# Projections for the gated recurrence taken inside it, in units of 128 columns, one head ahead

## What is computed

```python
    q_l, k_l, v_l, r_f, r_b, z_gla = ...            # 4 heads, dk 128, dv 256; z_gla 1024 wide
    la = log_sigmoid(r @ w_decay + b_decay) / 16    # per direction
def step(s, inp):                                    # _gla_scan, chunked
    bcum = jnp.cumsum(ac, axis=2)
    o_inter = jnp.einsum('bhtd,bhde->bhte', qc * jnp.exp(bcum), s)
    att = jnp.einsum('bhtd,bhsd,bhtsd->bhts', qc, kc, decay)
    o_intra = jnp.einsum('bhts,bhse->bhte', att, vc)
    s_new = jnp.exp(b_last[:, :, 0, :])[..., None] * s + jnp.einsum('bhsd,bhse->bhde', kc * jnp.exp(b_last - bcum), vc)
    br_c = (_rmsnorm(gla_o, gla_g_l).reshape(b_, t_, GLA_DV) * jax.nn.silu(z_gla)) @ w_br_gla_l
```

## Time and profile before

| | us |
|---|---|
| runs, median of 3 (range) | 2614.88 (2614.45 to 2615.42) |
| the profiled execution, device time | 2613.92 |
| its span, first to last instruction | 2612.1 |
| PE busy in the span | 2375.4 (91%) |
| DVE, ACT busy | 1527.6, 960.3 |

### The profile page before, as it was taken

How to read it: one execution, slowest core, us unless ns; L and a number is a source line. 1 busy time by engine, 2 the same in 40 slices (tenths; PEclk the granted TensorE clock), 3 DMA queues, 4 the chain that set the end, 5 groups by cost and what they waited for, 6 DMA issues and landing times.

```text
span 2612.1 us, 33657 instructions
## 1 busy us (share of the span) xinstructions
PE 2375.4 (91%) x13234; PEld 2070.6 (79%) x13234; DVE 1527.6 (58%) x2790; ACT 960.3 (37%) x1493; POOL 30.6 (1%) x37
## 2 busy tenths in 40 slices
PE   8899999999999777699988999998997669979997
PEld 6789988789888677688866888887786659949996
DVE  7879967789964355542344434454443455455665
ACT  5654535655442233222223321222333324334342
POOL 0000000000000000000000000000000100000000
PEclk9899989999989777799978999999998679989998
DMA  5258746178743100023210333332231005405552
GB/s 191 81 175 267 255 129 195 51 232 262 231 162 90 47 1 1 2 81 97 81 33 2 98 96 96 99 97 95 65 111 44 1 1 158 133 0 154 174 181 89
DMA packets 154709, 284.60 MB, mean 109 GB/s; under 512 B 9460, under 2 KB 34164, under 8 KB 154296
## 3 DMA queue, kind: packets, MB, share of 16 engines
q1 hardware_dynamic: 152448, 276.60, 34.0%
q10 hardware_dynamic: 2104, 5.85, 0.6%
HBM read 281.37 MB, written 1.05 MB: 108 GB/s over the span
## 4 chain that ended last, share of the span: by engine, by line
PE 75%; DVE 14%; DVEq 4%; ACT 4%; issue 2%; DMA 1%; ACTq 0%; SPq 0%
PE bank L1713 19%; PE bank L1714 19%; PE bank L1715 19%; DVE WLO L845 3%; PE bank L2065 2%; PE bank L2064 2%; PE bank L2117 1%; PE bank L1918 1%; PE bank L2134 1%; PE bank L2226 1%; PE bank L2246 1%; PE bank L2143 1%; DVEq L1261 1%; DVE ARENA L1258 1%; DMA RAW<-in_e_w_in 1%
## 5 line engine op out<-in xcount | busy, mean ns | idle before, releaser
L845 DVE TENSOR_TENSOR WLO<-RAW,WHI 128x1024 fp32r<-128x1024 f32 (+2 forms) x500 | 583.3, 1172 | 614.0 <-ACT WHI L453 601.9
L453 ACT ACTIVATE WHI<-RAW 128x1024 fp32r<-128x1024 f32 (+2 forms) x500 | 508.0, 1017 | 1092.9 <-PE bank L1715 1063.7
L1713 PE MATMUL bank<-ATH,WHI 128*128 128x256 f32 (+1 forms) x2032 | 655.3, 322 | 7.2 <-DVE ARENA L1400 2.6
L1714 PE MATMUL bank<-ATL,WHI 128*128 128x256 f32 (+1 forms) x2032 | 652.6, 321 | 0.0
L1715 PE MATMUL bank<-ATH,WLO 128*128 128x256 f32 (+1 forms) x2032 | 652.4, 321 | 0.0
L1713 PEld LDWEIGHTS bank<-ATH,WHI 128*128 128x128 f32 x2032 | 388.0, 191 | 40.0 <-DVE h L900 2.2
L1714 PEld LDWEIGHTS bank<-ATL,WHI 128*128 128x128 f32 x2032 | 387.9, 191 | 28.4
L1715 PEld LDWEIGHTS bank<-ATH,WLO 128*128 128x128 f32 x2032 | 387.8, 191 | 28.1
L1713 PE MATMUL bank<-WHI,ATH 128*128 128x512 f32 (+2 forms) x772 | 297.0, 385 | 12.3 <-DVE WLO L845 5.1
L1714 PE MATMUL bank<-WLO,ATH 128*128 128x512 f32 (+2 forms) x772 | 293.8, 381 | 0.0
L1715 PE MATMUL bank<-WHI,ATL 128*128 128x512 f32 (+2 forms) x772 | 293.2, 380 | 0.0
(11 more groups left out here) (277 smaller groups left out, 2820.8 us busy)
## 6 DMA issues: line engine op xcount, KB each, us to landing
RAW<-in_w_in SPq DMA_DIRECT2D x192, 512.0 KB, 3.6
RAW<-in_w_ff SPq DMA_DIRECT2D x128, 512.0 KB, 4.8
ARENA<-in_w_ada SPq DMA_DIRECT2D x64, 384.0 KB, 5.0
RAW<-in_o_w_in SPq DMA_DIRECT2D x24, 512.0 KB, 3.8
RAW<-in_e_w_in SPq DMA_DIRECT2D x16, 512.0 KB, 4.8
RAW<-in_w_ple_gate SPq DMA_DIRECT2D x16, 512.0 KB, 3.9
RAW<-in_w_br_gla SPq DMA_DIRECT2D x16, 512.0 KB, 3.5
RAW<-in_w_br_attn SPq DMA_DIRECT2D x16, 512.0 KB, 3.5
```

What stands on the lines that cost most here:

```text
L453: nc.scalar.activation(WHI[:, slot, 0:n], RAW[:, slot, 0:n], ACT.Copy).then_inc(hi_split, 1)
L845: V.tensor_tensor(WLO[:, slot, 0:n], RAW[:, slot, 0:n], WHI[:, slot, 0:n], ALU.subtract).then_inc(lo_split, 1)
L1713: mm(o, ah, bh, start=start, stop=False, skip_group_check=free)
L1714: mm(o, ah, bl, start=False, stop=False, skip_group_check=free)
```

## The change

It replaces the segments gq, gv and zg by a segment gh of five quads. Quads 0 to 3 belong to one head each: slot 0 holds 128 columns of q weights over all 1024 rows, slots 1 and 2 the head's 256 columns of v weights (512 rows each), slot 3 128 columns of z weights. Quad 4 holds the other four units of z. PE computes a unit of columns in two halves of 12 matmuls (`columns`) and values in four tiles of 24 (`value_tile`) in banks 2 and 3, placed by hand between the steps of the head before. ACT copies each piece out of PSUM (`taken`, semaphore piece_out), where DVE did so. z goes to ZRAW unactivated, its sigmoids are taken in a row behind the recurrence, and DVE forms silu, the products and the splits (`gate_z`) beside the first two quads of mgc. The GLA now has banks 0 and 1 for tiles and levels (4 to 7 for scores, states and outputs), turns rows into banks 6 and 7, and runs a head's turn and levels 0 to 2 before the head before it has ended; a level's scores run up to two levels behind its sums.

```diff
+    def tall(w, c0):
+        return (w, (lambda i: 0), (lambda i: c0), KC, P)
+
+    def head(w, i):
+        values = [(w, (lambda _, r=r: r * D // 2), (lambda _: C_GV + i * GDV), KC // 2, GDV) for r in range(2)]
+        return [tall(w, C_GQ + i * GDK)] + values + [tall(w, C_ZG + i * P)]
...
-            (f"gk{n}", 1, [std(w, C_GK)]), (f"gq{n}", 1, [std(w, C_GQ)]), (f"gr{n}", 1, [std(w, C_R, width=P)]),
-            (f"gv{n}", 2, [std(w, C_GV, BLK)]), (f"zg{n}", 2, [std(w, C_ZG, BLK)]),
+            (f"gk{n}", 1, [std(w, C_GK)]), (f"gr{n}", 1, [std(w, C_R, width=P)]),
+            (f"gh{n}", 1, [head(w, i) for i in range(GH)] + [[tall(w, C_ZG + (GH + u) * P) for u in range(SLOTS)]]),
             gated("mgc", 2, io["w_br_gla_2"][layer]),
...
+        ZRAW = [WG] + [a[:, i * TOK:(i + 1) * TOK] for a, i in ((GK, 0), (GK, 1), (GK, 2), (GQ, 0), (GQ, 1), (GQ, 2), (GK, 3))]
+        GC = [P1.rearrange("p k d n -> p (k d) n"), G[1]]
...
+                def gla_level(i, n):
+                    if n >= 2:
+                        act.wait_ge(g_level, (layer * GH + i) * (1 + len(LEVELS)) + n)
+                    if n == len(LEVELS) - 1:
+                        exps(LASTE[:, 0:tq], bank[0][:, 0:tq])
+                    else:
+                        for b in range(nb):
+                            exps(P2[:, n % 2, b, :, :], two(b if nb == 2 else n % 2))
...
+                def taken(q, u):
+
+                    act.wait_ge(gemm_step, steps0 + q * SLOTS + u + 1)
+                    b = bank[2 + u % 2]
+                    if u == 3 or q == GH:
+                        src, dst, scale = b[:, 0:tq], ZRAW[q if q < GH else GH + u][:, 0:tq], 1.0
+                    elif u == 0:
+                        src, dst, scale = b[:, 0:tq], GQ[:, q * TOK:q * TOK + tq], GDK ** -0.5
+                    else:
+                        src, dst, scale = b[:, :].rearrange("p (t n) -> p t n", t=2), VG[:, 2 * u - 2:2 * u, q * GDV:(q + 1) * GDV], 1.0
+                    nc.scalar.activation(dst, src, ACT.Copy, scale=scale).then_inc(piece_out, 1)
+
+                def next_hi(q, *slots):
+
+                    for slot in slots:
+                        act.wait_ge(gemm_step, steps0 + q * SLOTS + (3 if slot in (1, 2) and q < GH else slot + 1))
+                        hi_unit(slot, *order[pieces + q + 1][slot])
...
+                for i in range(GH - 1):
+                    taken(i, 3)
+                    next_hi(i, 3)
+                    gla_level(i, 2)
+                    gla_logs()
+                    for n in range(3, len(LEVELS)):
+                        gla_level(i, n)
+                    gla_tiles(0, 1)
+                    taken(i + 1, 0)
+                    next_hi(i + 1, 0)
+                    gla_tiles(2, 3)
+                    gla_turned()
+                    gla_level(i + 1, 0)
+                    taken(i + 1, 1)
+                    gla_level(i + 1, 1)
+                    taken(i + 1, 2)
+                    next_hi(i + 1, 1, 2)
...
+                act.wait_ge(g_turned, (layer + 1) * GH * 2)
+                act.drain()
+                for z in range(KC):
+                    nc.scalar.activation(SIGZ[:, z * TOK:z * TOK + tq], ZRAW[z][:, 0:tq], ACT.Sigmoid).then_inc(sig_done, 1)
...
+                        if j == 1 and b == 2:
+                            act.wait_ge(bt_ready, layer * 10 + 2)
...
                 for i in range(GH - 1):
-                    gla_head(i, True)
-                gla_head(GH - 1, False)
+                    gla_states()
+                    lo(1)
+                    gla_place(0)
+                    gla_place(1)
+                    gla_level(2, i)
+                    gla_place(2)
+                    gla_logsig()
+                    for n in range(3, 6):
+                        gla_level(n, i)
+                        gla_place(n)
+                    gla_level(6, i)
+                    gla_decays()
+                    gla_place(6)
+                    gla_place(7)
+                    lo(1)
+                    gla_keys(i + 1)
+                    gla_squares()
+                    gla_level(0, i + 1)
+                    gla_rows()
+                    gla_level(1, i + 1)
+                    gla_gains(i)
+                    lo(2)
...
+                def gate_z(i):
+                    w = SIGZ[:, i * 4 * TOK:(i + 1) * 4 * TOK].rearrange("p (c n) -> p c n", c=4)[:, :, 0:tq]
+                    for c in range(4):
+                        dve.wait_ge(sig_done, T.next(sig_done))
+                        V.tensor_tensor(w[:, c, :], w[:, c, :], ZRAW[4 * i + c][:, 0:tq], ALU.mult)
+                        if c % 2:
+                            lo(1)
+                    drain()
...
+                def columns(q, u, half):
+
+                    if half == 0:
+                        unit(u)
+                        if q or u >= 2:
+                            pe.wait_ge(*(outside(q, u - 2) if u >= 2 else outside(q - 1, u + 2)))
+                    for c in range(4 * half, 4 * half + 4):
+                        w = slice(c * P, (c + 1) * P)
+                        last = product(bank[2 + u % 2][:, 0:tq], WHI[:, u, w], WLO[:, u, w], ATH[:, c, 0:tq], ATL[:, c, 0:tq], c == 0, c == KC - 1)
+                    if half:
+                        last.then_inc(gemm_step, 1)
...
+                    for c in range(KC):
+                        slot, w, tk = 1 + c // 4, slice(c % 4 * GDV, (c % 4 + 1) * GDV), slice(t * P, (t + 1) * P)
+                        last = product(bank[3 - t // 2][:, t % 2 * GDV:(t % 2 + 1) * GDV], ATH[:, c, tk], ATL[:, c, tk],
+                                       WHI[:, slot, w], WLO[:, slot, w], c == 0, c == KC - 1)
+                    if t % 2:
...
+                def gla_tiles(i, *which):
+                    for b in which:
+                        exps_done(i, max(b - 1, 0))
...
-                        whole = bank[2 * n % 4 + b][:, :]
+                        exps_done(i, 4 + (n - 1) * 2 + b + 1 if nb == 2 else 3 + n)
+                        whole = bank[b if nb == 2 else n % 2][:, :]
...
+                    if m == 0:
+                        pe.wait_ge(g_kc, T.next(g_kc))
+                    else:
+                        pe.wait_ge(g_pair, T.next(g_pair))
+                    if m >= 2:
+                        pe.wait_ge(g_att, (layer * GH + i) * (1 + len(LEVELS)) + m - 1)
...
                 for i in range(GH - 1):
-                    gla_head(i, True)
-                gla_head(GH - 1, False)
-                loop_blocks(2, lambda: cols_product(4, AT, tq))
+                    gla_outer(i)
+                    columns(i, 3, 1)
+                    gla_inter()
+                    gla_scores(0, i)
+                    gla_scores(1, i)
+                    pe.wait_ge(*outside(i, 3))
+                    gla_pre(i + 1)
+                    gla_scores(2, i)
+                    gla_level(i, 3)
+                    gla_level(i, 4)
+                    gla_scores(3, i)
+                    gla_scores(4, i)
+                    gla_level(i, 5)
+                    gla_scores(5, i)
+                    gla_level(i, 6)
+                    gla_scores(6, i)
+                    pe.wait_ge(g_min, layer * GH + i + 2)
+                    columns(i + 1, 0, 0)
+                    pe.wait_ge(g_la, T.next(g_la))
+                    gla_tiles(i + 1, 0, 1)
+                    columns(i + 1, 0, 1)
+                    gla_scores(7, i)
+                    gla_tiles(i + 1, 2, 3)
+                    value_tile(i + 1, 0)
+                    gla_values(i)
+                    gla_turn()
+                    gla_level(i + 1, 0)
+                    value_tile(i + 1, 1)
+                    gla_level(i + 1, 1)
+                    gla_level(i + 1, 2)
+                    value_tile(i + 1, 2)
+                    gla_rows()
+                    value_tile(i + 1, 3)
+                    columns(i + 1, 3, 0)
+                i = GH - 1
+                gla_outer(i)
+                columns(i, 3, 1)
+                gla_inter()
+                gla_scores(0, i)
+                gla_scores(1, i)
+                columns(GH, 0, 0)
+                gla_scores(2, i)
+                gla_level(i, 3)
...
+                gla_rows()
+                pe.wait_ge(g_normed, T.next(g_normed))
+                pe.wait_ge(*outside(GH, 3))
```

More of the change, by code:

```diff
@@ new lines, in _ @@
+                pieces = [n for n, _ in quads].index(f"gh{layer}")
+                steps0 = T.now(gemm_step)
+                def taken(q, u):
[8 more added lines that the diff above has]
+                    nc.scalar.activation(dst, src, ACT.Copy, scale=scale).then_inc(piece_out, 1)
@@ new lines, in _ @@
+                gla_states()
+                lo(1)
+                gla_place(0)
+                gla_place(1)
+                for n in range(2, 5):
+                    gla_level(n, GH - 1)
+                    gla_place(n)
+                lo(1)
+                gla_level(5, GH - 1)
```

(35 more changed lines are left out.)

214 lines of the change are left out of this document (125 added, 89 removed).

## The result

| us | before | changed | ratio (95% interval) |
|---|---|---|---|
| median (range) of 4 runs each | 2614.66 (2608.74 to 2615.42) | 2500.64 (2498.21 to 2503.91) | 0.9567 (0.9551 to 0.9582) |
| span of the profiled execution | 2612.1 | 2499.1 | |

The account below looks back on a forecast made before the run. Bound by TensorE, with empty time and half clock in the two gated recurrences. Layer 0's 73.4 us less and layer 1's 43.3 took 116.7 off 2613.9, giving 2497.2, stated as 2498; own range 2487 to 2509.

Parts of the forecast that it names:

- wait for bt_ready: Gate quads: second sigmoid waits for the second split on DVE, 1.4 us in layer 0, some 3 in layer 1.
- slow start of the gate quads: Gate quads behind the recurrence start at half clock: +1.9 us in layer 0, +1 in layer 1.
- step 3: Full heads' remaining PE waits: logs 4.1 us (layer 0), 4.9 (layer 1); states 0.4 and 1.4; g_la 1.1 in layer 1.
- step 4: Half clock behind the log wait in full heads: +3 us in layer 0 (bounds 0, +8.8), +2.5 in layer 1 (0, +5.6).
- A: Rival: waits for the logs leave the clock at 1.00, no clock is lost; 2476 us, chance 0.17.
- B: Rival: clock falls at every log wait and stays low until the next 512-column piece; 2521 us, chance 0.21.
- steps 5 and 6: Recurrence stage's ends: opening to first outer product 40 us in layer 0, 36 in layer 1; last head 55 and 34.
- The signs: Right: heads 60 to 64 and 46 to 50 us, PE over 88% busy. Wrong: heads above 68, product clock below 0.85.
- Rival C: Queues in order: one missed wait per head on a weight split or copy, 8 us in six heads; 2546, chance 0.11.
- Rival D: Slower: projections in the recurrence suffer the heads' slow clock, PE work there taking 1.37 times; 2625 us, chance 0.03.
- step 7: Silu, products and splits beside the gate quads cost nothing, but a sigmoid wait (1.4, 3 us) and half-clock start (+1.9, +1).
- Rival E: Nothing is hidden, because each projection piece is waited for where it stands; 2615 us, chance 0.02.

Follow-up runs that it names:

- experiment 1: Changed kernel with the Ln of the logs replaced by another Exp, so its table loads go and the decays become other numbers: 2476.82 us.
- 2: Changed kernel with the logs divided, the exps of level 3 standing between their Exp and Ln: 2480.95, 2487.42 and 2492.79 us.
- 3: Changed kernel with the whole of the logs behind the exps of level 3 on ScalarE: 2499.59 us.
- experiment 5: Changed kernel plus 32 useless product matmuls ahead of scores(4) in each full head of layer 1: 2488.20 us.
- Experiment 8: Changed kernel with divided logs, gate_z's split ahead of its weight split, and value tiles and half units moved at both ends of the stage: 2459.98 us.
- experiment 4: Changed kernel with column units and value tiles of segment gh thinned to 2 of their 8 terms, result incomplete: 2434.09 us.
- 7: Changed kernel with divided logs; in layer 1 gla_pre writes banks 3 and 7 and a half unit stands before scores(5): 2471.80 us.
- 9: Changed kernel with all edits of 7 and Experiment 8 together: 2451.75 us, ratio to before 0.9382.
- 6: Changed kernel with the split into BTH and BTL ahead of the third weight split in gate_z on VectorE: 2496.19 us.

## Why the prediction was right

It was right in the total, in the mechanism and in nearly every term. In part it was luck: the stages' errors (+4.1 and -2.6 us) cancel, and so do those of wait and clock within a head.

| term, us | said | measured |
|---|---|---|
| opening, layer 0 / 1 | 40 / 36 | 42.7 / 34.8 |
| full head, layer 0 / 1 | 62.7 / 48.2 | 63.0 / 48.2 |
| last head | 55 / 34 | 54.0 / 32.8 |
| wait for bt_ready | 1.4 / 3 | 1.5 / 2.2 |
| slow start of the gate quads | 1.9 / 1 | 3.3 / 1.5 |
| stages in all | 286.4 / 218.6 | 290.5 / 216.0 |

The measured column comes from the times of the first matmul of each part; the slow start is 46.35 us of gate products less 192 x 0.224, and 24.7 less 192 x 0.121.

- **The log wait (step 3).** Said 4.1 at level(4) and 4.9 at scores(4); measured 3.88 and 4.62. Experiments 1 to 3 show its cause: it shrinks when the table loads go, divides with the logs and moves with them.
- **Other waits.** The states' 0.4 in layer 0 did not show, the 1.4 in layer 1 was exact. The 1.1 for g_la in layer 1 was not there: the half clock behind the log wait slows TensorE, and hides it. In experiment 5, with the clock kept, 0.89 of it appears.
- **The clock (step 4).** Taken at +3 and +2.5. In layer 0 the half clock lies over these stretches of the first, second and third head:

```profile
861.20:871.30 10.10, 7.63 (x36) 7.63 (x36) 4.29 (x8) 3.96 (x6) 0.00 (x0) 0.50 0.00 0
926.20:932.80 6.60, 5.92 (x28) 5.93 (x28) 1.72 (x5) 1.50 (x4) 0.00 (x0) 0.50 0.00 0
987.60:997.60 10.00, 8.36 (x39) 8.36 (x40) 4.61 (x10) 3.15 (x5) 0.00 (x0) 0.50 0.00 0
```

  In the first, everything from 863.67 to 871.4 took twice its time: the sums of a level 3.5 us, the scores of two levels 3.4 and part of the next sums. That costs 3.9, and by the same reckoning the others cost 3.0 and 4.2. Taken off the heads (63.2, 62.4, 63.5), this leaves 59.3 or 59.4 in each: 3.9 of wait and 55.4 of work, where 4.8 and 54.9 were said. In layer 1 the clock cost 3.9: 48.2 less 38.3 of work as said less 6.0 of waits. So the price of the clock was too low by some 0.7 and 1.4, and the waits were too long by 0.9 and 1.4; that is why the heads came out right.
- **Rivals A and B.** A is out (the clock fell in every head of both executions traced). B's first half came true, but its second half is out: the clock came back at 871.4 in the middle of level sums, not with the next 512-column piece, and doubled 3.9 us of work and not 8.8. The trace of before could have told against A. The prediction says that it bears on no idle of 4 us inside a head, but it has one of 5.88 in the first full head of layer 1, behind which the clock is at 0.50:

```profile
2034.05 0.58 PE L2064 MATMUL bank<-BTH,BTL 128*128 128x256 f32 x1 [5.88 <-DVE BTL L1429]
...
2028.20:2032.30 4.10, 0.00 (x0) 0.00 (x0) 1.59 (x3) 3.67 (x3) 0.00 (x0) 0.96 0.00 0
...
2034.00:2038.00 4.00, 3.78 (x16) 3.49 (x16) 3.06 (x16) 1.93 (x4) 0.00 (x0) 0.50 0.00 0
```

- **The ends (steps 5 and 6).** The opening of layer 0 was 2.7 us too short: its last half unit took 4.55 us (840.38 to 844.93) where 2.75 is its price at full clock, and a wait of 1.32 at level 2 was missing in the walk. Experiment 8, without the waits, is 6.6 us shorter there.
- **The signs.** TensorE was to be busy over 88% of the heads: it is 93.7% in layer 0 and 87.5%, just short, in layer 1. The stages took 290.5 and 216.0 where some 286 and 219 were said. Of the signs of being wrong one shows, in a single piece: most of the opening's last half unit in layer 0 ran at half clock (840.8 to 844.0).
- **Elsewhere.** The stages gave 115.2 us (621.7 less 506.5), the span 113.0. The difference is the later start, 3.35 us, which is there before any changed instruction, less 1.1 behind.
- **Rival C** (a missed wait on a weight split or copy in each head) has no row. **Rival D** is out: a half unit takes 3.0 us with the drain of its last matmul in every head, so the projections kept their price. What it took from the earlier trace rows, the mean clock of 0.75, belonged to heads with empty time in them. Its counter-argument was too strong, though: the first 512-column products of zg, from 1113.0 to 1117.5, ran at 0.53, as step 7 itself says. **Rival E** is out by the total.

What experiment 4 adds: it divides the gain of a head in two. In layer 1 17.4 us of projections cost a head only 6.8 (48.2 against 41.4), a gain of 10.6, and 8.6 of it is the filling (13 us left out save 4.4). In layer 0 22.4 us cost 4.7, a gain of 17.7; there the filling is 8.0 (16.8 left out save 8.8). The other 2.0 and 9.7 are the steps moved up and what the projections left in place (4.4 and 5.6 us) still hide; no run parts these two.

## What to carry to other kernels

When stages are interleaved, walk the in-order queue of each engine and not TensorE's alone: the largest wait left inside the heads came from a 6 us block on ScalarE, which TensorE's own queue does not show, and dividing that block was worth 8 to 20 us. Price a wait on TensorE by what it does to the clock behind it too: here 3.9 us of waiting cost 3.0 to 4.2 more. Work put in such a wait may cost less than nothing, and where no bank is free for it, one pair of outputs in other banks may free it.

## What the runs showed that was not expected

- Useless matmuls made the kernel faster: 3.9 us more per head in three heads, 7.4 us less time in them.
- The clock fell after waits as short as 1.08 us, and not always. In layer 0: in 2 of 3 heads after 1.08 to 1.09 (experiment 1), in 1 of 3 after 1.30 to 1.31, in each of 2, 7, 8 and 9. In layer 1: in 1 of 6 after 1.37 to 1.40 at scores(5) (7 and 9), in all 3 after 2.54 (1), in all 6 after 2.87 (2 and 8). After 3.88 and 4.6, in all 12 of the two executions of the changed kernel. So a head's time is not fixed by its waits (57.2 or 61.9). The Trainium skill, "TensorE: Matmul & The Clock Gate", in its section on what is actually happening in the clock gate, says that the number of slow matmuls at a kernel's start varies with the gate's phase. No run here tests a start, and whether the third head's 61.9 against 57.2 is of that kind is not shown; that it is the third in four traces speaks against mere chance.
- In experiment 5 3.8 us were won in an attention without any edit, in 6 some 1.5 lost. Differences of that size between variants are read from the stage that was edited, not from the total.
